# Reversed token streams and interleaved weight halves in the dense stages of a two-block transformer kernel

## What is computed

```python
def swiglu(h, w_gate, w_up, w_down):
    return (jax.nn.silu(h @ w_gate) * (h @ w_up)) @ w_down

f, nq, nk, nv, cq, ckv, kr, g = jnp.split(h @ lp['w_in'], IN_OFFSETS, axis=-1)
proj = jnp.einsum('bngi,gio->bngo', y, w_branch)
return jnp.sum(gate * proj, axis=2) @ w_out
```

## Time and profile before

| | before |
|---|---|
| median of 3 runs | 3154.04 us |
| range of the runs | 3150.85 to 3156.76 us |
| the profiled execution's own time | 3151.03 us |
| its span, first to last instruction | 3149.2 us |
| mean granted TensorE clock over the span | 0.958 of 2.4 GHz |
| PE busy | 2893.3 us, 92% |
| PEld (weight loads) busy | 2306.7 us, 73% |
| DVE busy | 1686.4 us, 54% |
| ACT busy | 1209.5 us, 38% |
| DMA, mean | 105 GB/s |

### The profile page before, as it was taken

The page is one execution under the profiler, slowest core; times in us unless marked ns, Lnnn a source line. Parts: engine busy times, 40 slices in busy tenths (PEclk is TensorE's granted clock), DMA queues, the critical chain, the costliest instruction groups (busy, mean ns, idle before and its releaser), DMA issues. The chain is left out here.

```text
span 3149.2 us, 37052 instructions
## 1 busy us (share of the span) xinstructions
PE 2893.3 (92%) x14705; PEld 2306.7 (73%) x14705; DVE 1686.4 (54%) x2379; ACT 1209.5 (38%) x1800; POOL 453.8 (14%) x445
## 2 busy tenths in 40 slices
PE   7998899999979999999799799998999978876995
PEld 4886566888868888888587457886888846555774
DVE  3385665233355666642515563446656454655997
ACT  5324555122243211221534443324323244635774
POOL 4400200000040000002500100002000124122332
PEclk9999899999989999999899899999999989897997
DMA  7650101222113444431620103333656326335962
GB/s 213 131 167 19 25 1 51 61 61 66 52 51 104 142 126 134 140 96 33 109 65 16 25 11 91 100 85 110 191 172 190 110 39 83 155 90 187 377 237 81
DMA packets 397871, 330.11 MB, mean 105 GB/s; under 512 B 38038, under 2 KB 340484, under 8 KB 397572
## 3 DMA queue, kind: packets, MB, share of 16 engines
q1 hardware_dynamic: 384196, 304.56, 33.1%
q0 software_dynamic: 13248, 23.13, 3.1%
q10 hardware_dynamic: 256, 0.07, 0.0%
HBM read 331.96 MB, written 30.33 MB: 115 GB/s over the span
## 5 line engine op out<-in xcount | busy, mean ns | idle before, releaser
L1191 PE MATMUL ps<-ahi,w_hi 128*128 128x512 f32 (+1 forms) x2264 | 766.4, 352 | 5.2 <-DVE w_lo L1218 5.2
L1192 PE MATMUL ps<-ahi,w_lo 128*128 128x512 f32 (+1 forms) x2264 | 766.1, 352 | 0.0
L1218 DVE TENSOR_TENSOR w_lo<-w_raw,w_hi 128x1024 fp32r<-128x1024 f32 (+2 forms) x242 | 340.6, 1409 | 365.6 <-ACT w_hi L1208 363.5
L1191 PEld LDWEIGHTS ps<-ahi,w_hi 128*128 128x128 f32 x2264 | 428.0, 189 | 69.0 <-DVE w_lo L1218 7.5
L1194 PE MATMUL ps<-alo,w_hi 128*128 128x512 f32 (+1 forms) x2264 | 472.9, 351 | 0.0
L1192 PEld LDWEIGHTS ps<-ahi,w_lo 128*128 128x128 f32 x2264 | 428.4, 189 | 59.2 <-issue 0.2
L1208 ACT CAST w_hi<-w_raw 128x1024 fp32r<-128x1024 f32 (+2 forms) x244 | 285.6, 1171 | 461.6 <-PE ps L1194 366.7
L1194 PEld LDWEIGHTS ps<-alo,w_hi 128*128 128x128 f32 x2264 | 377.6, 189 | 56.7
L944 DVE SCALAR_TENSOR_TENSOR vec_acc<-vec_w,csilu,vec_acc 128x512 f32<-128x512 f32 x364 | 255.2, 747 | 8.3 <-DVE vec_acc L944 5.5
L1358 POOL TENSOR_TENSOR xsum<-x 128x768 f32<-128x768 f32 (+1 forms) x4 | 6.3, 1567 | 1407.0 <-DVE x L1337 1407.0
L1281 DVE SCALAR_TENSOR_TENSOR x<-ps,mod,x 128x512 f32<-128x512 f32 x80 | 51.4, 668 | 232.3 <-PE ps L1194 219.3
(11 more groups left out here) (556 smaller groups left out, 5231.6 us busy)
## 6 DMA issues: line engine op xcount, KB each, us to landing
vec_w<-in_w_mod SPq DMA_DIRECT2D x128, 512.0 KB, 4.0
w_raw<-in_w_in SPq DMA_DIRECT2D x102, 512.0 KB, 3.9
e_raw<-in_w_gate SPq DMA_DIRECT2D x46, 512.0 KB
e_raw<-in_w_up SPq DMA_DIRECT2D x46, 512.0 KB
e_raw<-in_w_down SPq DMA_DIRECT2D x46, 512.0 KB
w_raw<-in_w_ffn_gate SPq DMA_DIRECT2D x44, 512.0 KB, 4.4
w_raw<-in_w_ffn_up SPq DMA_DIRECT2D x44, 512.0 KB, 3.7
w_raw<-in_w_ffn_down SPq DMA_DIRECT2D x32, 704.0 KB, 4.4
```

Of the source, the lines that this page charges most:

```text
L1191: pe.matmul(o, whi[:, j, b0 + b, :], hi[:, b, t0:t0 + tn], start=(b == 0), stop=False)
L1192: pe.matmul(o, wlo[:, j, b0 + b, :], hi[:, b, t0:t0 + tn], start=False, stop=False)
L1218: dve.tensor_tensor(wlo[:, j, 0:d.blocks, :], raw_of(d, i, jj), whi[:, j, 0:d.blocks, :].bitcast(F32), ALU.subtract).then_inc(lo_ready[j]. ...
```

## The change

Two places differ. In the last form of the inner loop, both the output in PSUM and the moving operand are read with a step of -1: the last token streams first. In the ring, `w_hi` and `w_lo` become one tile, `w_parts`, in which the high and the low value of each weight stand side by side. A block's 128 high values are then 128 words with a step of two words, over 1024 bytes, and so are its low values. The gap puts the ring at 128 modulo 256 instead of 0; since the raw tile is a multiple of 256 bytes long, `w_parts` begins at 128 modulo 256 as well. Each engine issues the same instructions in the same order as before; only access patterns and addresses differ. The two waiting forms of the inner loop keep their forward streams, but take their weights from the new tile too. ScalarE's copy now writes with a step of two words; VectorE's subtraction reads the high part and writes the low part with that step.

```diff
                             else:
+
                                 for t0, tn in groups(d.T):
-                                    o = bank(t0, tn)
+                                    o = bank(t0, tn)[:, ::-1]
                                     for b in range(nb):
-                                        pe.matmul(o, whi[:, j, b0 + b, :], hi[:, b, t0:t0 + tn], start=(b == 0), stop=False)
-                                        pe.matmul(o, wlo[:, j, b0 + b, :], hi[:, b, t0:t0 + tn], start=False, stop=False)
+                                        high = hi[:, b, t0:t0 + tn][:, ::-1]
+                                        pe.matmul(o, whi[:, j, b0 + b, :], high, start=(b == 0), stop=False)
+                                        pe.matmul(o, wlo[:, j, b0 + b, :], high, start=False, stop=False)
                                     for b in range(nb):
-                                        m = pe.matmul(o, whi[:, j, b0 + b, :], lo[:, b, t0:t0 + tn], start=False, stop=(b == nb - 1))
+                                        m = pe.matmul(o, whi[:, j, b0 + b, :], lo[:, b, t0:t0 + tn][:, ::-1], start=False, stop=(b == nb - 1))
...
         def new_ring(c, blocks):
-            place(c, 0)
-            return (sb(c, "w_raw", [P, 2, blocks, P]), sb(c, "w_hi", [P, 2, blocks, P], F32R), sb(c, "w_lo", [P, 2, blocks, P], F32R))
+
+            place(c, 128)
+            raw, parts = sb(c, "w_raw", [P, 2, blocks, P]), sb(c, "w_parts", [P, 2, blocks, P, 2], F32R)
+            return raw, parts[:, :, :, :, 0], parts[:, :, :, :, 1]
```

## The result

The change makes the kernel slower. Before: 3155.4 us median of 4 runs (3150.85 to 3157.07). After: 3187.83 us median of 4 (3184.98 to 3188.08). The ratio is 1.0109, 95% interval 1.0096 to 1.0121, or 30 to 38 us. The forecast was 3070 us and faster, within 3035 to 3185 us; the time lies 3 us above the upper end of the range.

What follows compares the result with a forecast made beforehand. The prediction took PE, busy 92% of 3149.2 us, to bound the kernel. It summed 3151.0 - 103.8 + 19 = 3066, plus 3.0 us from profiled execution to median, forecasting 3070 us, range 3035 to 3185.

Steps and rivals of the forecast that it cites:

- What bounds the kernel, and where the effect would be: PE, busy 92% of 3149.2 us; the changed loop is 1800 us of it, and in it PE waits for nobody.
- The first term: Loop L1191 to L1194: weight and token reads kept apart save 11.0 ns on each of 9414 matmuls, together -103.8 us.
- all 13.3 ns: Loss per full-rate matmul over its column stream, at 512 and 256 columns; winning all was the gain's upper bound, 125 us.
- The slack value: Matmul pace without meetings, from the float32 transposes' 2 to 3 ns loss: 215.6 ns at 512 columns, 109 at 256.
- The nine matmuls with four weight columns: Trace row at 0.231 us each; should be near 214 if a load's reads caused the loss.
- The rival of wrong phase: Loop: weights read first column first, so reversed tokens make more meetings; +125 + 19, about 3298 us; chance 0.09, 0.08 slower.
- the rival with fixed pace and visible splits: Loop: 13.3 ns is a fixed cost of changing weights, only splits show; 3173 us, up to 3217; chance 0.25.
- The splits: Writing high and low weight parts with a step of two: ACT +0.6 us, DVE +0.65 us per 128x1024.
- The sum of +19 us: Longer splits show where PE already waits for `w_lo`: 15 x 1.25 us, bounds 0 to 38.
- The nearest row for ScalarE: L1254 writes 512 elements in 589 ns in one piece, up to 1217 with a step of eight words; 1.2 ns more an element.
- The rule on ports: Skill rule: TensorE has two independent read ports, weight loads take no SBUF bandwidth from the running matmul; first term 0.

Runs made afterwards that it cites:

- `sweep_sep`: Kernel before, each of eight rings at its own place modulo 256, parts apart, each second chunk reversed; 227.1 to 236.1 ns per 512-column matmul.

## Why the prediction was wrong

**What bounds the kernel, and where the effect would be: right.** Nearly the whole difference is the pace of the loop's 9414 matmuls (32.5 of 34.0 us), without a new wait.

**The first term, -103.8 us, is the step that failed.** It said: "the load's reads of SBUF and the stream's meet", and the change "is a way to keep them apart". Measured in its place: +32.5 us, 6276 x 6.1 ns (227.4 to 233.5) less 3138 x 1.8. Two things in it were wrong.

*The size of what could be won.* I took all 13.3 ns as avoidable save 2.3. (The term's arithmetic is off by a trifle: 6276 x 11.0 ns is 69.0 us, not 69.3.) In 32 cells of place, direction and step and in all changes of operands, no mean with real tokens came below 226.7 ns at 512 columns. The slack value itself was well judged: 216.7 ns with one-word tokens, against my 215.6. But a stream at this rate doesn't get there by moving the weights.

*The old place was taken for an arbitrary one.* I asked what the change would mend and not what it would break. Forward streams with weights in one piece at a distance of 0 modulo 256 is the best place that was found; every other distance, direction or step that was tried costs 0.6 to 10 ns at 512 columns. Moving ring and tokens together keeps it.

**The evidence against, misread.** The nine matmuls with four weight columns at 231 ns I read as "no faster than with 128 columns". They are 4 ns slower than the chunk of the earlier trace rows, and that was the useful fact. Their weights aren't at the old place either (in the built program the high tile begins at 224 modulo 256, the low one at 96), so that place and number of columns were mixed; at the old place four columns measured 231.1 and at place 224 a full block 233.1. Each alone is enough for such a pace. The row spoke for a pace that can get worse, which I gave 0.08.

**The rival of wrong phase was right in its sign and in what would show it (233 ns and more), wrong in its price.** It said +125 us, the loss doubled at every matmul; the runs don't show whether its reason (weights read first column first) is so. The loss rose by half at 512 columns (13.3 to 20 ns) and fell slightly at 256 (13.3 to 11.2). My argument against it, that reads at different rates meet in any phase and so leave little room, doesn't stand: the ring at 128 alone costs +1.0%. The range took 3173 to 3185 only from the rival with fixed pace and visible splits, which was wrong in mechanism.

**The splits: right in direction for ScalarE, too high in size for both.** ScalarE +0.11 us per 1024 elements (1154 against 1047 ns), taken as 0.6, bounds 0 to 1.25. VectorE 1267 against 1270 ns, taken as +0.65: nothing. The sum of +19 us for waits on `w_parts` measured about 0, as the rows above show. The nearest row for ScalarE (a step of eight words) was much too far from a step of two.

The Trainium skill's rule in Vector Engine (DVE) Microarchitecture Reference, section 5.2, gave an estimate of 1.8 to 2.6 us for this split. The trace doesn't agree for a step of two words in one input and the output: 1.27 us, as before.

**The rule on ports.** A full weight load costs the stream no more than one of four columns, so the load's reads don't take the stream's cycles one by one. But moving the weights 128 bytes against the tokens costs 1% and moving both nothing, so the stream's pace does depend on where the weights lie. That the two reads collide is the reading that fits; no run shows the collision itself. By the Trainium skill's rule (TensorE: Matmul & The Clock Gate, Part 2, step 1) the first term would have been 0 and the time 3173 us: nearer than mine, and still without the 32.5 us that the pace lost. The trace bears out the half on the amount of reads, and not independence of place.

**What stays open.** Why forward streams at distance 0 run at 226.7 ns; what else moves the other geometries by up to 3 ns at the same addresses; why most other geometries come to a mean of 233.3; and why one word of distance counts differently from the two sides. Every one of these is a measured pattern without a shown mechanism. A matmul without any weight load ahead of it was not tried.

## What to carry to other kernels

When a tuned loop runs at an even pace (here 226.7 ns, in layer 1 nearly without scatter), treat its addresses as part of the tuning: before moving a ring or turning a stream, vary the place alone and read the distance of starts. One kernel with another place in each stage gives a first curve in one run; since stages at the same addresses differed by up to 3 ns, a place that looks good has to be tried in the whole kernel. And keep the distance modulo 256 between weights and tokens when an allocation ahead of them changes size, for 128 bytes of it cost 1% here.

## What the hardware showed beyond the prediction

- fp32r tokens with a step of two words stream at half rate: 451 ns for 512 columns, 227 for 256, at the full clock.
- Tokens from one word stream at 216.7 ns, 3.4 above the columns' own time. Tokens in one piece never had a mean below 226.7 in a stage.
- A weight block with a step of two words loads in 195 ns instead of 188 to 189 and 256 columns stay at 120; with a step of four it takes 315 ns and they stand at 233.
- Many means stand at a loss of 8, 32 or 48 cycles of 2.4 GHz per matmul (216.7, 226.7 and 233.3 ns at 512 columns). Distances that differ from one matmul to the next can still average 233.3: in `sweep_sep`, forward, mostly 235 and 232 in turn at 32, and 231 and 236 at 64.
- With the stream reversed, or with 4-byte steps of its place, the 256-column matmuls move apart from the 512-column ones: the old place is best for 512 and among the worst for 256 (120 ns, against 113.5 at 64 bytes).
